# Second block's attentions: the products of the sixteen meta keys with 128 rows and 128 stationary columns

## The reference, cut to what matters

```python
h = jnp.concatenate([meta, x, zeros], axis=1)            # 16 meta tokens, then the sequence
...
decay = cum[:, :, q0:q0 + Q_BLOCK, None] - cum[:, :, None, :kend]
return jnp.where(kpos[None, :] <= qpos[:, None], s + decay, NEG_INF)
...
p = jax.nn.softmax(s, axis=-1).astype(v.dtype)
outs.append(jnp.einsum('bhqk,bkhd->bqhd', p, v[:, :kend]))
...
y = jnp.concatenate([fox, mla], axis=-1) @ w_out
return x + _rmsnorm(y, norm_post)                         # the rows behind the meta tokens are returned
```

## Time and profile before

| | |
|---|---|
| median of 3 runs | 2986.29 us |
| lowest and highest | 2979.86 and 2986.85 us |
| span of the profiled execution | 2980.6 us (its own time is not listed) |
| TensorE, mean granted clock of the span | 0.986 |
| GpSimd's fills, then first pair of the latent attention | from 2599.46 us on |
| first product of the first pair's values, first third | 2234.23 us |

### The profile page before, as it was taken

One profiled execution on the slowest core, in us unless ns is written; L12 is line 12 of the kernel. 1 busy time (PEld: TensorE's weight loads), 2 busy tenths in 40 slices (PEclk: granted clock), 3 DMA queues, 4 the chain that ended last, 5 costly groups with the idle time before them and its releaser, 6 DMA issues.

```text
span 2980.6 us, 36188 instructions
## 1 busy us (share of the span) xinstructions
PE 2870.9 (96%) x13519; PEld 2235.7 (75%) x13536; DVE 1507.4 (51%) x1789; ACT 947.7 (32%) x1536; POOL 803.3 (27%) x498
## 2 busy tenths in 40 slices
PE   6999999999999999999999999999999999999998
PEld 5888885666577776778888888887787777877766
DVE  6454556644543336454334444333426665377764
ACT  4322226655600003231212211122224444254441
POOL 5312203422333331113332332331121111221225
PEclk8999999999999999999999999999999999999999
DMA  5200100000111111001111111111201001000023
GB/s 191 92 22 22 43 8 15 22 21 19 66 49 47 43 44 36 29 15 57 43 49 49 46 46 49 48 43 43 85 23 37 16 22 26 11 6 6 16 102 118
DMA packets 166337, 128.57 MB, mean 43 GB/s; under 512 B 19264, under 2 KB 150048, under 8 KB 165968
## 3 DMA queue, kind: packets, MB, share of 16 engines
q1 hardware_dynamic: 164816, 118.55, 13.2%
q10 hardware_dynamic: 1408, 8.50, 0.7%
HBM read 114.20 MB, written 12.65 MB: 43 GB/s over the span
## 4 chain that ended last, share of the span: by engine, by line
PE 86%; DVE 7%; ACT 2%; issue 1%; DMA 1%; POOL 1%; SPq 0%; ACTq 0%; DVEq 0%; POOLq 0%
PE ps L753 21%; PE ps L754 20%; PE ps L755 20%; PE ps L2854 2%; PE ps L2570 2%; PE ps L2694 2%; PE ps L2561 2%; PE ps L665 1%; PE ps L2492 1%; PE ps L2553 1%; PE ps L2462 1%; PE ps L2749 1%; DVE max_parts L2116 1%; PE ps L2950 1%; PE ps L2951 1%
## 5 line engine op out<-in xcount | busy, mean ns | idle before, releaser
L753 PE MATMUL ps<-NH,w_high 128*128 128x512 f32 (+2 forms) x1992 | 771.1, 387 | 13.8 <-POOL w_low L1111 8.0
L754 PE MATMUL ps<-NL,w_high 128*128 128x512 f32 (+2 forms) x1992 | 772.8, 388 | 0.0
L755 PE MATMUL ps<-NH,w_low 128*128 128x512 f32 (+2 forms) x1992 | 769.5, 386 | 0.0
L1109 POOL CAST w_high<-w_raw 128x1024 fp32r<-128x1024 f32 x193 | 208.9, 1082 | 1939.3 <-PE ps L755 1166.8
L1111 POOL TENSOR_TENSOR w_low<-w_raw,w_high 128x1024 fp32r<-128x1024 f32 x193 | 481.8, 2496 | 15.5
L753 PEld LDWEIGHTS ps<-NH,w_high 128*128 128x128 f32 x1992 | 376.4, 189 | 101.6 <-issue 10.7
L755 PEld LDWEIGHTS ps<-NH,w_low 128*128 128x128 f32 x1992 | 376.7, 189 | 76.8
L754 PEld LDWEIGHTS ps<-NL,w_high 128*128 128x128 f32 x1992 | 375.8, 189 | 77.3
L858 DVE TENSOR_TENSOR hT<-hT,ps 128x1024 f32<-128x1024 f32 x168 | 205.0, 1221 | 227.5 <-PE ps L755 227.5
L753 PE MATMUL ps<-act_high,w_high 128*128 128x512 f32 x352 | 141.5, 402 | 2.9 <-DVE act_low L1997 2.9
L755 PE MATMUL ps<-act_high,w_low 128*128 128x512 f32 x352 | 139.2, 396 | 0.0
(11 more groups left out here) (410 smaller groups left out, 5261.5 us busy)
## 6 DMA issues: line engine op xcount, KB each, us to landing
w_raw<-in_w_in SPq DMA_DIRECT2D x69, 512.0 KB, 3.8
w_raw<-in_w_up SPq DMA_DIRECT2D x44, 512.0 KB, 3.8
w_raw<-in_w_out SPq DMA_DIRECT2D x24, 512.0 KB, 3.4
w_raw<-in_w_down SPq DMA_DIRECT2D x22, 512.0 KB, 3.7
w_raw<-in_w_xkv SPq DMA_DIRECT2D x8, 512.0 KB, 5.6
x_in<-in_x SPq DMA_DIRECT2D x8, 512.0 KB, 9.2
residual_spill<-hT SPq DMA_DIRECT2D x1, 4096.0 KB, 13.6
hT<-residual_spill ACTq DMA_DIRECT2D x1, 4096.0 KB, 13.1
```

The costliest lines, as they stand in the source:

```text
L753: nc.tensor.matmul(o, wh, xh, start=start, stop=False)
L754: nc.tensor.matmul(o, wh, xl, start=False, stop=False)
L755: return nc.tensor.matmul(o, wl, xh, start=False, stop=stop)
L1109: nc.gpsimd.tensor_copy(WH[slot][:, :], w_raw[slot][:, :]).then_inc(w_high, 1)
```

## The change

Score products of a meta block read 128 stationary columns, those of the 16 meta keys and of the 112 keys behind them, and write all 128 partitions of their bank; ScalarE and VectorE still take 16 rows of it. The value products of a meta block take all 128 partitions of tile NT and of the buffers `PH` and `PL`. For that, tile NT is filled with zeros behind the meta values (in `VH` its first 16 partitions get their ones back), and the eight buffers `PH` and `PL` are filled with zeros twice: on VectorE ahead of `query_low(0)`, and on GpSimd behind the fills of L1163, once the last norm ahead of the latent attention has made its low part (`n_lo`). ScalarE waits on the new semaphore `p_clear` for each of the two, ahead of the copies of the first pair's queries and ahead of those of the first latent pair's values.

```diff
--- before.py
+++ after.py
@@ -487,6 +487,7 @@
                              "p_numerator_ready", "p_dve_step", "p_out_ready"))
         p_exp, p_lo, p_vh, p_vm = (
             sem(x) for x in ("p_exp_done", "p_low_ready", "p_v_high_ready", "p_meta_v_high_ready"))
+        p_clear = sem("p_parts_cleared")
         f_qh, f_kh, f_kl, f_qk = (
             sem(x) for x in ("f_q_high_ready", "f_k_high_ready", "f_k_low_ready", "f_qk_parts_ready"))
         p_rows = [sem(f"p_rows_landed{h}") for h in range(2)]
@@ -1162,6 +1163,10 @@
                         pool.wait_ge(m_filled, 8 * s_ + 4 * h + n) if s_ + h + n else None
                         nc.gpsimd.memset(to[s_][h][96:P, :].bitcast(F32), value).then_inc(m_filled, 1)
             pool.wait_ge(m_filled, 16)
+            pool.wait_ge(n_lo, NORM["kvm"][2] + 1)
+            for t_ in PH + PL:
+                r = nc.gpsimd.memset(t_[:, :].bitcast(F32), 0.0)
+            r.then_inc(p_clear, 1)
 
             def finish(pm, half):
 
@@ -1505,6 +1510,7 @@
 
             for n in range(4):
                 act.wait_ge(k_out[n], 32)
+            act.wait_ge(p_clear, 1)
             for pb in range(4):
                 J, U = 6 * pb, FOX_UNITS * pb
                 wait_done(act, FOX, 0, J)
@@ -1600,6 +1606,7 @@
             norm_high(act, "kvm", 0)
             for j in (KN, QP, KVM):
                 m_high(0, j)
+            act.wait_ge(p_clear, 2)
             for pm in range(4):
                 pb = pm + 4
                 m_high(pm, VN)
@@ -2055,10 +2062,17 @@
                                                        QS[h][0:HD, :].bitcast(F32), ALU.mult, ALU.subtract)
                 r.then_inc(job_free[FOX.slot(6 * pb)], 1)
 
+            for t_ in PH + PL:
+                nc.vector.memset(t_[:, :].bitcast(F32), 0.0)
+            nc.vector.memset(VL[:, 0:NT, HD:P].bitcast(F32), 0.0)
+            nc.vector.memset(VL[:, NT, :].bitcast(F32), 0.0)
+            nc.vector.memset(VH[:, 0:NT, HD:P].bitcast(F32), 1.0)
+            nc.vector.memset(VH[:, NT, :].bitcast(F32), 0.0).then_inc(l_dve, 1)
+            dve.wait_ge(l_dve, 4)
+            nc.vector.memset(VH[0:META, NT, HD:P].bitcast(F32), 1.0).then_inc(l_dve, 1)
+            dve.wait_ge(l_dve, 5)
+            nc.vector.sem_inc(p_clear, 1)
             query_low(0)
-            nc.vector.memset(VL[:, :, HD:P].bitcast(F32), 0.0)
-            nc.vector.memset(VH[:, :, HD:P].bitcast(F32), 1.0).then_inc(l_dve, 1)
-            dve.wait_ge(l_dve, 4)
             nc.vector.memset(QX[0][HD:HD + 2, :].bitcast(F32), 1.0)
             nc.vector.memset(QX[1][HD:HD + 2, :].bitcast(F32), 1.0).then_inc(k_set, 1)
 
@@ -2727,9 +2741,9 @@
                         pe.wait_ge(p_rows[h], pb * 32 + 32)
                         own = j >= 0 and j // 4 == half
                         c0 = (j % 4) * P if own else 0
-                        ks, rows = (slice(0, META), META) if j < 0 else (slice(META + j * P, META + (j + 1) * P), P)
+                        ks = slice(0, P) if j < 0 else slice(META + j * P, META + (j + 1) * P)
                         qs = slice(half * HALF + c0, (half + 1) * HALF)
-                        mm = passes(b[0:rows, c0:HALF], second_pass(h, ks, qs), own)
+                        mm = passes(b[:, c0:HALF], second_pass(h, ks, qs), own)
                         if own:
                             mm = nc.tensor.matmul(b[:, c0:c0 + P], identb, m_k, start=False, stop=True)
                         mm.then_inc(unit_done, 1)
@@ -2743,12 +2757,12 @@
                         pe.wait_ge(p_lo, pb * 28 + (n + 3))
                         c0 = (j % 4) * P if j >= 0 and j // 4 == half else 0
                         vc = slice(0, P) if h == 0 else slice(HD, MW)
-                        rows, t = (META, NT) if j < 0 else (P, j)
+                        t = NT if j < 0 else j
                         o = pair[st.slot(k_u + h)][:, half * HALF + c0:(half + 1) * HALF]
-                        ph, pl = (t_[n % 4][0:rows, c0:HALF] for t_ in (PH, PL))
-                        nc.tensor.matmul(o, VH[0:rows, t, vc], ph, start=(j < 0), stop=False)
-                        nc.tensor.matmul(o, VH[0:rows, t, vc], pl, start=False, stop=False)
-                        nc.tensor.matmul(o, VL[0:rows, t, vc], ph, start=False, stop=(j == 3 + 4 * half)).then_inc(p_pv, 1)
+                        ph, pl = (t_[n % 4][:, c0:HALF] for t_ in (PH, PL))
+                        nc.tensor.matmul(o, VH[:, t, vc], ph, start=(j < 0), stop=False)
+                        nc.tensor.matmul(o, VH[:, t, vc], pl, start=False, stop=False)
+                        nc.tensor.matmul(o, VL[:, t, vc], ph, start=False, stop=(j == 3 + 4 * half)).then_inc(p_pv, 1)
 
             for pb in range(4):
                 J, U = 6 * pb, FOX_UNITS * pb
```

## The result

The changed kernel takes 2990.95 us (median of 20 runs, 2984.55 to 2996.18), the kernel before 2985.62 us in 20 runs (2974.49 to 2986.85). The ratio is 1.002 with a 95% interval of 1.0014 to 1.0027, so 4 to 8 us longer; the forecast was 1.7 us longer, 2988, in a range of 2979 to 2995. The profiled execution took 2991.39 us, with a span of 2989.6.

A forecast was written before the change was run, and what follows sets the result against it. TensorE was taken as the bound, busy 96% of the span and 86% of the chain that ended last. Stall 7.9 plus clock 1.9 less gain 8.1 gave +1.7 us on the median 2986.3: 2988 us, range 2979 to 2995.

The forecast's parts named there:

- the steps of 0.23 us: TensorE's value products of the meta keys with 128 rows, each 0.23 us behind the one before, loads ahead of them.
- the gap: TensorE standing still about 8 us in the forgetting attention's first projection of values.
- the half clock behind it: TensorE at 0.50 of its clock after its stall in the first values' projection, costing 1.9 us (bounds 1.5 and 2.5).
- the other three pairs about 1 us shorter each: Forgetting pairs after the first would each be about 1 us shorter in the profile, latent pairs as well.
- part 1: Value products of the meta keys: 128 rows save 0.40 us in each of 32 groups, 12.8 us at most.
- Rival (a): Value products: row count costs nothing, open loads have another cause; +11.1 us, 2997, slower; chance 0.05.
- part 2: Of the value products' 12.8 us, 3.4 is lost in waits for other engines, leaving 9.4 (half lost: 6.4).
- part 3: Score products of the meta keys: 128-column loads stand open behind 13 waits, 0.1 us each, 1.3 us lost.
- part 4: VectorE's fills ahead of the first pair stall TensorE 7.9 us (7.3 to 8.5), and lowered clock adds 1.9.
- part 5: GpSimd's fills ahead of the latent attention: 0.55 us each, 4.4 in all, hidden, cost 0.
- (b): GpSimd's fills go by partitions, 1.9 us each, 15.2 in all, delaying TensorE; +10.9 us, 2997, slower; chance 0.05.
- (c): No TensorE stall, as VectorE's fills or the low part end in time; -8.1 us, 2978; chance 0.05.

The follow-up runs named there:

- 64 rows: Changed kernel with VectorE's eight large fills moved to its idle time and the value products of the meta keys at 64 rows instead of 128: 2985.81 us, ratio 1.0005.
- the fills alone: Changed kernel with all its fills and waits, but every product as in the kernel before (16 rows, 16 stationary columns): 2995.75 us, ratio 1.0041.
- the score products alone: Kernel before with 128 stationary columns in the score products of the meta keys and nothing else: 2985.59 us, ratio 1.0002.
- the fills later: Changed kernel with VectorE's small fills behind the queries' low part and its eight large ones where it stood idle: 2984.94 us, ratio 1.0004 to the kernel before.
- the value products alone: Changed kernel with VectorE's fills moved later and score products of the meta keys kept at 16 stationary columns: 2978.06 us, ratio 0.9979 to the kernel before.
- TensorE kept busy in the stall: Changed kernel with 32 unused products of 512 columns in TensorE's stall ahead of the first pair's values: 2987.42 us, ratio 1.0012 to the kernel before.
- longer pairs: 128-row value products, 16-column score products, fills moved later, plus five idle products ahead of block 8 of each forgetting pair: 2981.33 us, ratio 0.9987.
- with the wait covered: Six idle products in the 1.43 us wait, fills moved later: whole change 2977.99 us (ratio 0.9975), 128-row value products without wide score products 2975.08 us (0.9965).

## Why the prediction was right, point by point

The forecast of no measurable change (within 0.3%) held, at the upper side: 4 to 8 us longer for 1.7. It held by the width of its range; the size of the change was off, since the interval leaves out 1.7 and reaches past the bound of +5.9. Three terms were sized well, one too large, and one is missing. Of the signs that the prediction named, the steps of 0.23 us, the gap and the half clock behind it came; "the other three pairs about 1 us shorter each" did not.

- **Value products** (part 1): 0.40 us forecast for a group, 0.39 in the timeline, with the loads ahead of their products as it needs. Rival (a) is out: 128 rows take the idle time away and 64 rows bring it back in full. The rule of the Trainium skill (TensorE: Matmul & The Clock Gate, Part 3, The mechanism) by which a load runs ahead only where its row group differs (the Trainium skill's paragraph above it adds "or the background weight buffer", which the prediction left out) doesn't by itself describe this kernel: its loads run ahead where the row count stays and stand still where it changes.
- **What reaches the end** (part 2): right for the forgetting attention, where a pair at full clock gained 0.96 us (four groups of 0.40, less the 0.40 that runs into block 19's low part and some 0.2 for the score products). Too large for the latent attention, by one group in each pair: a pair gained 0.67, where the terms give 1.0 to 1.1. Two rows of the changed kernel's second latent pair show where it stays:

```profile
2719.67 0.42 PE L2868 MATMUL ps<-NH 128*128 128x344 f32 x1 [0.90 <-DVE max_parts L2334]
...
2745.26 0.44 PE L2940 MATMUL ps<-probs_high,v_high 128*128 128x384 f32 x1 [0.22 <-DVE probs_low L2308]
```

Block 0's gain turned into a longer wait for the maxima, 0.90 us for the 0.52 of the earlier trace rows, as forecast. Block 14's went in part into a new wait of 0.22 for block 16's low part, a loss of the kind that I had counted for the forgetting attention and not here. With 0.96 and 0.67 for each of four pairs, an estimate of the whole gain is 6.5 us, not 8.1.

- **Score products** (part 3): 1.3 forecast. Pairs at full clock give 0.16 us for a forgetting pair and 0.10 for a latent one (67.35 to 67.25), 1.0 in all by an estimate. Alone the edit costs 0.8, its interval reaching to both sides of zero.
- **VectorE's fills** (part 4): stall 7.41 for 7.9, half clock 2.33 for 1.9, in sum 9.7 for 9.8; the fills alone cost 10.6 in the medians. That the sum came so close is luck in part: one piece was too large by 0.5, the other too small by 0.4.
- **GpSimd's fills** (part 5): 0.48 us each for 0.55, hidden. Rivals (b) and (c) are out.
- **The missing term**: the sum takes a shortened pair as a gained one. The second and third pair gave their 1 us back at half clock behind a wait that the kernel before has too (the third lost 0.78 more to a wait for the rows of the maxima). In the profiled execution they are 1.0 and 1.7 us over the first, and the stretch of the fourth is 1.8 over the one before where it should be 1.0 under it: 5.5 us in all. With the other terms, 9.7 - 6.5 + 5.5 = +8.7, against the spans' difference of 9.0. This match is luck in part: 1.2 us of the 9.0 lie ahead of the first new fill (2229.96, where the low part stood at 2228.76), and about 1.0 comes back behind the fourth stretch (377.4 us to the end for 381.1, 3.7 less, where four latent pairs give 2.7). From the first pair's transposes to the end the changed kernel is only 1.9 us shorter (735.8 for 737.8), so of the gain of 8.1 in the sum less than a quarter reached the end of this execution; by the prediction's own rule, a gain off by more than twice, the step that takes saved time as gained time failed. By the medians, the part given back is about 2 us (9.7 - 6.5 = 3.2, against 5.3). But the profiled execution of the kernel before is a quick one: with a span of 2980.6 it took an estimated 2982.4 us (the changed kernel's time is 1.8 over its span), 3.2 under the median of its runs.

**What stays open.** When the wait of 1.43 us brings the half clock. The same two waits stand at the start of the pairs in all kernels without a cover. Call a pair caught where the clock falls behind them. The profiled executions with value products of 16 or 64 rows (the kernel before, the fills alone, 64 rows, the score products alone) have no caught pair; all five with 128 rows have one at least: the third pair always, the first never, the second and the fourth in three (the changed kernel, the fills later, the value products alone) and not in two (TensorE kept busy in the stall, longer pairs). So the changed products matter, but neither the wait nor the length of the pair decides alone: a pair of 80.71 us kept full clock, and one lengthened to about 81.6 was caught. It may hang on when the wait falls; no run here varies that by itself.

Open too is why the whole change with the fills later took 7 us more than the value products alone (2984.94 to 2978.06) and 2.9 us more with the wait covered: the profiled pairs differ by 0.2 us, the score products alone cost 0.8, and the runs of the whole change are spread over 11 us. The two traces explain a part. Their spans differ by 4.4 us (2980.7 to 2976.3); 1.8 of that lie ahead of the first pair's transposes (2246.34 to 2244.57), where both do the same work, and 1.7 in the stretch of the fourth pair (111.65 us at a mean clock of 0.97, 109.91 at 0.98). So most of these 4.4 us don't lie in the wide products' own time. The five longest runs of the whole change show a lower mean clock (0.980) than the others (0.982 to 0.984), but only one of its executions was profiled, and none of those.

## What to carry to other kernels

Keep the row count of the stationary operand the same from product to product: padding with zeros took 0.39 us from the group shown, while the group's own pace stayed at 0.23 us. A fill put in front of the first step of a chain costs that chain's whole delay; the same eight fills cost 4.3 us of an engine that stood idle some 10 us later, and there nothing of the time (from the start of the queries' low part to the first pair's transposes 14.08 us, 14.09 in the kernel before). And on an engine with a varying clock a saved microsecond counts only when the clock holds: here the version with the lowest median, 2975.08 us, 0.35% under the kernel before, needed the value products alone, the fills moved, and a wait of 1.43 us filled with idle products.

## What the runs showed that I had not expected

A wait of 1.43 us, shortly behind one of 0.51, was followed by half clock (a mean of 0.57 over 4 us) in some pairs with value products of 128 rows and by full clock in others, in the first pair of every run among them; six idle products in it kept the clock at 1.00 in all pairs. Operands of 64 rows between those of 128 cost as much as those of 16, 4.0 us for 16 loads. And GpSimd clears 128 partitions of 512 columns in 0.48 us, about half of what it needs for 32 partitions of 1024: in these two shapes the time goes by columns.
